# Two activation parts in one 512-column product, with the halves of the bank summed on VectorE

## The chip, the cores and the metric

The kernel runs on one core of one Trainium2 chip. The metric is the device time of one execution in microseconds. Engines are named as the profile names them: PE is TensorE (PEld its weight loads), DVE is VectorE, ACT is ScalarE, POOL is GpSimd, SP is SyncE. They run at once, each through its own list of instructions in order, and wait for one another on semaphores.

## The reference

Two transformer blocks over 256 tokens of width 1024, in float32. The change touches two places of the first block: the "up" half of its feed-forward layer (which runs twice, once in each of two layers) and the input projection of a short convolution.

```python
def dwconv3(x, w):
    xp = jnp.pad(x, ((0, 0), (1, 1), (0, 0)))
    return xp[:, :-2] * w[0] + xp[:, 1:-1] * w[1] + xp[:, 2:] * w[2]

def conv_ffn(a, w_up, conv_w, w_down):              # D_FF = 2816
    g, u = jnp.split(dwconv3(a @ w_up, conv_w), 2, axis=-1)
    return (jax.nn.silu(g) * u) @ w_down

def short_conv_mixer(a, w_in, conv_w, w_out):       # w_in is 1024 x 3072
    gate_b, gate_c, u = jnp.split(a @ w_in, 3, axis=-1)
    return (gate_b * dwconv3(gate_c * u, conv_w)) @ w_out
```

After this block come attention and a mixture of 32 experts, which take the second half of the time and which the change leaves alone.

## The kernel before, in words

**Products in three parts.** Activations lie transposed: 128 features on the partitions, 256 tokens along the free dimension, KC = 8 chunks of features. For precision each weight and each activation is split in two numbers, hi (rounded to fp32r) and lo (what is left), and a product is made as w_hi·a_hi + w_hi·a_lo + w_lo·a_hi, all summed in PSUM. `split_tile` makes one tile of 128 output features: for each of the 8 chunks a 256-column product with a_hi (L2127) and one with a_lo (L2128), then eight with w_lo (L2131). So w_hi's block is loaded twice for each chunk, and one tile is 24 products of 256 columns.

**Weight items.** Weights come by DMA in items of 1 MB (128 x 2048 in SBUF), into a ring of six cells. ACT rounds each item to `wd_hi` (`round_item`, L809) and DVE subtracts it to get `wd_lo` (`split_item`, L1337). Both have two buffers, so item k+2 can be split only when the tiles of item k are done, and the tile's L2131 products wait for DVE's part. One item holds the two tiles of one step of the loop below.

**The up loop** (`ffn` on each engine, FC = 22 steps j, two layers). Step j has a gate tile (s = 0) and a value tile (s = 1). PE makes both into two of six PSUM banks (`ffn_bank`). ACT multiplies each by the convolution's middle tap into SBUF (`center`, L961). DVE adds the two outer taps, shifted by one token, reading the tile from PSUM (`shifts`, L1561 and L1564, for the gate and then for the value). ACT takes the silu of the gate (L973), POOL multiplies gate and value (L742), ACT rounds that product (L955) and DVE makes its rest (L1554). The order within a step is written out by hand, and it is what the prediction is about. On ACT: center gate, center value, wait for the gate's two taps, silu, round weight item j+2, round the product of step j-1. On DVE: the four taps, the lo part of item j+2 (waits for ACT's rounding), the rest of step j-1. The last two steps split the first two items of the down half in place of up items.

**The short convolution** has 8 steps of three tiles (B, C and u): ACT copies C out of PSUM (L1000), DVE multiplies it with u (L1605), ACT applies the middle tap (L1004), DVE the outer ones (L1607, L1610), and DVE multiplies with B (L1616). In two of the steps DVE and ACT also split an item in the middle (`SC_BETWEEN`).

**The wide form** exists already for other matrices: `wide_tile` (L2144) multiplies w_hi with a_hi and a_lo side by side in one 512-column product, which fills a bank with two halves of 256 columns, and adds w_lo·a_hi to the second half (L2147). Whoever reads the tile adds the halves.

Of the kernel before, what the change touches and what calls it, by code (L numbers as in the profile page):

```python
# [129 lines left out]

SPLIT_STAGES = ("qkv", "win_out", "up0", "down0", "sc_in", "sc_out", "up1", "down1", "w_in", "w_out", "gate")
# [31 lines left out]
def build(nc, wdense, wmoe, small_d, tab_d, tab2_d, x_d, ctx_d, p_d, wg_d, wr_d, bup_d, bdown_d, out_d):  # L163
    with ExitStack() as stack:
# [136 lines left out]
        ctx_in, ctx_sq, ctx_sum, ctx_root = sem("ctx_in"), sem("ctx_sq"), sem("ctx_sum"), sem("ctx_root")  # L301
# [7 lines left out]
        FFN_COUNTS = dict(up=2 * FC, center=2 * FC, shift=4 * FC, silu=FC, act=FC, act_hi=FC, act_lo=FC, fed=9, right=KC, down=KC)  # L309
# [6 lines left out]
        sc_proj, sc_c, sc_cu, sc_center = sem("sc_proj"), sem("sc_c"), sem("sc_cu"), sem("sc_center")  # L316
        sc_shift, sc_mix, sc_out = sem("sc_shift"), sem("sc_mix"), sem("sc_out")

# [5 lines left out]
        def ffn_bank(j, s):  # L324
            return ps[:, 2 * (j % 3) + s, 0:T]
# [399 lines left out]
        def _(pool):  # L725
# [61 lines left out]
        def _(act):  # L787
# [57 lines left out]
            def window_qkv():  # L845
# [25 lines left out]
                def ctx_root_():  # L871
                    act.wait_ge(ctx_sum, 8)
                    act.activation(rstd[:, T:TT], ps[:, 6, 0:T], ACT.Sqrt, bias=eps[:, 0:1]).then_inc(ctx_root, 1)
# [76 lines left out]
            def ffn(L):  # L950
# [6 lines left out]
                def center(j, s):  # L957
                    act.wait_ge(*ffn_at(L, "up", j * 2 + s + 1))
                    if j >= 2:
                        act.wait_ge(*ffn_at(L, "act", j - 1))  # L960
                    act.activation(ffn_buf(s, j % 2), ffn_bank(j, s), ACT.Copy, scale=conv(L, 1, s)[:, j:j + 1]).then_inc(ffn_sem["center"], 1)  # L961

                bring_in(ACT.Silu, L)
                for j in range(FC):
# [7 lines left out]
                    act.wait_ge(*ffn_at(L, "shift", j * 4 + 2))  # L972
# [13 lines left out]
            def short_conv():  # L986
# [4 lines left out]
                for n in range(KC):  # L991
# [5 lines left out]
                    act.wait_ge(sc_proj, 3 * n + 1)  # L997
                    if n >= 2:
                        act.wait_ge(sc_mix, n - 1)
                    act.activation(sc_buf(0, b), ps[:, 3 * b, 0:T], ACT.Copy).then_inc(sc_c, 1)  # L1000
# [307 lines left out]
        def _(dve):  # L1308
# [46 lines left out]
            def norm(n, src=None, first=None):  # L1355
# [20 lines left out]
                if n == 5:  # L1376
                    dve.wait_ge(root_taken, 1)
# [20 lines left out]
            def window_qkv():  # L1398
# [37 lines left out]
                dve.wait_ge(ctx_root, 1)  # L1436
# [112 lines left out]
            def ffn(L, after):  # L1549
# [6 lines left out]
                def shifts(j):  # L1556
                    for s in range(2):
                        y, c = ffn_bank(j, s), ffn_buf(s, j % 2)
                        dve.wait_ge(*ffn_at(L, "center", j * 2 + s + 1))

                        dve.scalar_tensor_tensor(out=c[:, 1:T], in0=y[:, 0:T - 1], scalar=conv(L, 0, s)[:, j:j + 1], in1=c[:, 1:T],  # L1561
                                                 op0=ALU.mult, op1=ALU.add).then_inc(ffn_sem["shift"], 1)
                        dve.wait_ge(*ffn_at(L, "shift", j * 4 + 2 * s + 1))
                        dve.scalar_tensor_tensor(out=c[:, 0:T - 1], in0=y[:, 1:T], scalar=conv(L, 2, s)[:, j:j + 1], in1=c[:, 0:T - 1],  # L1564
                                                 op0=ALU.mult, op1=ALU.add).then_inc(ffn_sem["shift"], 1)

                split_item(up, 2)
# [21 lines left out]
            def short_conv():  # L1589
                def rest(n):  # L1590
# [3 lines left out]
                for n in range(KC):  # L1594
# [4 lines left out]
                    dve.wait_ge(sc_c, n + 1)  # L1599
# [4 lines left out]
                    cu, o = sc_buf(1, b), sc_buf(2, b)  # L1604
                    dve.tensor_tensor(cu, ps[:, 3 * b + 1, 0:T], sc_buf(0, b), ALU.mult).then_inc(sc_cu, 1)  # L1605
# [192 lines left out]
            def route():  # L1798
# [13 lines left out]
                dve.wait_ge(root_taken, 2)  # L1812
# [300 lines left out]
        def _(pe):  # L2113
# [160 lines left out]
            def window_qkv():  # L2274
# [75 lines left out]
                pe.wait_ge(ctx_root, 1)  # L2350
# [83 lines left out]
            def ffn(L):  # L2434
                up, down = f"up{L}", f"down{L}"
                first_tiles([ps[:, t, 0:T] for t in range(4)], up, (0, 1), ffn_sem["up"], NORM_GROUPS[2 * L + 1])
# [5 lines left out]
                pe.wait_ge(*ffn_at(L, "shift", 4 * (FC - 2)))  # L2442
                pe.wait_ge(mod_ready, modulated(NORM_GROUPS[2 * L + 1]))
                for j in range(11):
# [34 lines left out]
            def short_conv():  # L2479
                first_tiles([ps[:, t, 0:T] for t in range(4)], "sc_in", (0, 1), sc_proj, NORM_GROUPS[2])  # L2480
                for n in range(4, 24):
                    m, kind = n // 3, n % 3
                    if m >= 2 and kind == 0:
                        pe.wait_ge(sc_mix, m - 1)
# [676 lines left out]
```

## Time and profile before

| | |
|---|---|
| median of 3 runs | 1839.61 us (1839.33 to 1845.45) |
| the profiled execution: its span | 1841.9 us, inside the range of the runs and 2.3 us over their median |
| PE / DVE / ACT / POOL busy | 97% / 41% / 33% / 4% |
| granted PE clock, mean | 0.991 |
| two up loops, steady part | 99.08 us each, 17 steps |

A busy share is an average over stages with different limits, and the starts and ends of matmuls overlap, so it doesn't say what sets the time of a stage. The chain of waits does: it is followed back from the last instruction to what released each one.

### The profile page before, as it was taken

To read this page: it belongs to the slowest core of one execution; us is meant where nothing else is said; L and a number is where in the kernel's file an instruction comes from. 1 tells how busy PE (TensorE), PEld (TensorE's weight loads), DVE (VectorE), ACT (ScalarE), POOL (GpSimd) and SP (SyncE) were. 2 spreads that over 40 slices of the span, in tenths; PEclk is the share of its full clock that TensorE was granted. 3 is DMA by queue.
4 is the path that set the end of the run, shared out by engine and by line. 5 is a ranking of instruction groups with operands and counts; after the bars stand their busy time and mean duration, and the time that the engine had idled before them with its cause. 6 is when DMAs were issued, how large, how long until landed. Compare 5 with 4: busy or idle time off the path is not lost.

```text
span 1841.9 us, 32831 instructions
## 1 busy us (share of the span) xinstructions
PE 1790.2 (97%) x13696; PEld 1328.3 (72%) x13696; DVE 753.5 (41%) x1603; ACT 611.9 (33%) x1096; POOL 82.1 (4%) x98
## 2 busy tenths in 40 slices
PE   6999999999999999999999999999999999999997
PEld 4764899989899989968656656566656666556556
DVE  3575677656677746475211112121112112111116
ACT  3457555544455536484111111111111111111115
POOL 0010111100111100101000000000000000000001
PEclk9999999999999999989999999999999999999999
DMA  9648745556465464526899999999999999999993
GB/s 393 255 166 328 282 173 180 205 181 235 180 249 179 167 212 155 178 114 249 356 424 424 425 423 426 423 426 424 426 395 422 426 427 427 425 427 424 427 423 123
DMA packets 64421, 580.59 MB, mean 315 GB/s; under 512 B 5968, under 2 KB 9552, under 8 KB 11056
## 3 DMA queue, kind: packets, MB, share of 16 engines
q1 hardware_dynamic: 63872, 577.17, 77.5%
q8 instruction: 91, 1.49, 0.3%
q10 hardware_dynamic: 432, 1.71, 0.3%
q14 instruction: 26, 0.21, 0.0%
HBM read 577.81 MB, written 1.05 MB: 314 GB/s over the span
## 4 chain that ended last, share of the span: by engine, by line
PE 74%; DVE 11%; DMA 8%; ACT 6%; issue 1%; ACTq 0%; DVEq 0%; SPq 0%
PE ps L2807 22%; PE ps L2820 11%; DVE wd_lo L1337 6%; PE ps L2716 5%; ACT wd_hi L809 5%; DMA ring<-in_experts 4%; PE ps L2456 4%; DMA ring<-in_weights 3%; PE ps L2832 3%; PE ps L2460 2%; PE ps L2131 2%; PE ps L2127 2%; PE ps L2128 2%; PE ps L2205 2%; PE ps L2793 2%
## 5 line engine op out<-in xcount | busy, mean ns | idle before, releaser
L2807 PE MATMUL ps<-ring,A 128*64 128x256 f32 x3840 | 431.4, 381 | 7.8 <-DMA ring<-in_experts 3.8
L2807 PEld LDWEIGHTS ps<-ring,A 128*64 128x64 f32 x3840 | 272.4, 137 | 162.7 <-issue 25.3
L1980 DVE TENSOR_TENSOR A<-ps,W 128x512 f32<-128x512 f32 x64 | 44.3, 692 | 730.1 <-PE ps L2793 730.1
L1337 DVE TENSOR_TENSOR wd_lo<-ring,wd_hi 128x2048 fp32r<-128x2048 f32 x103 | 235.8, 2291 | 166.8 <-ACT wd_hi L809 166.7
L809 ACT ACTIVATE wd_hi<-ring 128x2048 fp32r<-128x2048 f32 x107 | 204.0, 1907 | 128.1 <-PE ps L2460 65.2
L2127 PE MATMUL ps<-aL_both,wd_hi 128*128 128x256 f32 x944 | 232.7, 284 | 1.9 <-ACT wd_hi L809 1.4
L2128 PE MATMUL ps<-aL_both,wd_hi 128*128 128x256 f32 x944 | 231.4, 283 | 0.0
L2820 PE MATMUL ps<-ring,A 128*64 128x512 f32 x960 | 213.4, 595 | 1.3 <-DMA ring<-in_experts 1.3
L2127 PEld LDWEIGHTS ps<-aL_both,wd_hi 128*128 128x128 f32 x944 | 181.0, 192 | 4.2 <-issue 3.1
L2128 PEld LDWEIGHTS ps<-aL_both,wd_hi 128*128 128x128 f32 x944 | 181.1, 192 | 0.1
L1155 ACT ACTIVATE A<-ps 128x512 f32<-128x512 f32 x64 | 38.2, 597 | 396.2 <-PE ps L2807 377.5
L2820 PEld LDWEIGHTS ps<-ring,A 128*64 128x64 f32 x960 | 66.5, 137 | 123.6 <-issue 121.6
L2131 PE MATMUL ps<-aL_both,wd_lo 128*128 128x256 f32 x944 | 135.7, 286 | 0.8 <-DVE wd_lo L1337 0.2
L2131 PEld LDWEIGHTS ps<-aL_both,wd_lo 128*128 128x128 f32 x944 | 120.8, 191 | 2.8 <-DVE wd_lo L1337 2.0
L2716 PE MATMUL ps<-A 128*128 128x64 f32 x960 | 113.9, 272 | 0.0
L2716 PEld LDWEIGHTS ps<-A 128*128 128x128 f32 x960 | 111.9, 192 | 0.0
L1203 ACT ACTIVATE A<-ps 128x512 f32<-128x512 f32 x32 | 19.1, 597 | 202.8 <-PE ps L2820 192.5
L1175 ACT ACTIVATE A<-A 128x256 f32<-128x256 f32 x64 | 26.7, 417 | 171.6 <-DVE A L1985 171.6
L2456 PE MATMUL ps<-ff_both,wd_hi 128*128 128x512 f32 x320 | 76.3, 391 | 0.0
L2456 PEld LDWEIGHTS ps<-ff_both,wd_hi 128*128 128x128 f32 x320 | 58.8, 188 | 11.4
L2832 PE MATMUL ps<-A 64*128 64x256 f32 x512 | 63.9, 389 | 1.3 <-ACT A L1203 1.3
L2832 PEld LDWEIGHTS ps<-A 64*128 64x128 f32 x512 | 47.0, 186 | 18.2 <-issue 14.1
(436 smaller groups left out, 2179.3 us busy)
## 6 DMA issues: line engine op xcount, KB each, us to landing
ring<-in_experts SPq DMA_DIRECT2D x180, 2048.0 KB, 20.8
ring<-in_weights SPq DMA_DIRECT2D x161, 1024.0 KB, 5.1
aT<-in_experts SPq DMA_DIRECT2D x11, 2048.0 KB, 20.4
hT<-in_x SPq DMA_DIRECT2D x1, 1024.0 KB, 7.4
hT<-in_ctx SPq DMA_DIRECT2D x1, 1024.0 KB, 18.4
hT<-in_weights SPq DMA_DIRECT2D x1, 1024.0 KB, 8.6
tab<-in_tables ACTq DMA_DIRECT2D x1, 768.0 KB, 7.0
tab<-in_experts SPq DMA_DIRECT2D x1, 768.0 KB, 4.4
```

The source lines that it names most:

```text
L809: act.activation(wd_hi[:, split_buf(name, k)], w, ACT.Copy).then_inc(split_hi, 1)
L1155: act.activation(u[:, j, :], ps[:, 4 + j, :], ACT.Copy).then_inc(moe["u"], 1)
L1337: dve.tensor_tensor(wd_lo[:, b], cell(PLAN[name]["first"][k]["cell"]), wd_hi[:, b].bitcast(F32), ALU.subtract).then_inc(split_lo, 1)
L1980: dve.tensor_tensor(m_gl[:, j].rearrange("p c h n -> p (c h) n"), ps[:, TURN_BANKS[j], :].rearrange("p (c n) -> p c n", c=8), b_up[:, 8 * ...
L2127: pe.matmul(out, wd_hi[:, b, c, cols], a_hi[:, c, :], start=(c == 0), stop=False)
L2128: pe.matmul(out, wd_hi[:, b, c, cols], a_lo[:, c, :], start=False, stop=False)
L2131: mm = pe.matmul(out, wd_lo[:, b, c, cols], a_hi[:, c, :], start=False, stop=(c == KC - 1))
L2456: pe.matmul(halves(n), hi[:, k, n * P:(n + 1) * P], ff_both[:, :, kk], start=(kk == 0), stop=False)
L2716: mm = pe.matmul(ps[:, GATHER_BANK, c * CAP:(c + 1) * CAP], xt[:, s, c * P:(c + 1) * P], oh[:, s, :], start=(s == 0), stop=(s == 1))
L2807: mm = pe.matmul(ps[h * CAP:(h + 1) * CAP, 4 + j, q * T:(q + 1) * T], xg[:, c, :], block(c, h), start=(c == 0), stop=(c == KC - 1))
L2820: mm = pe.matmul(ps[h * CAP:(h + 1) * CAP, DOWN_BANK, :], m_act[:, 4 * kh + c, :], w[:, c, h], start=(kh == 0 and c == 0), stop=(kh == 1 a ...
L2832: mm = pe.matmul(ps[:, f // 2, (f % 2) * T:(f % 2 + 1) * T], y[rows, n * P:(n + 1) * P], ohT[rows, :], start=(first and n % 2 == 0), stop= ...
```

## The change

Up tiles and convolution input tiles are made with `wide_tile` (and `first_tiles` with wide=True for the first four): 8 products of 512 columns and 8 of 256 for each tile, in place of 24 of 256. The two halves of the bank are added by a DVE reduction out of PSUM into SBUF. In the up loop `center` and the taps then read that sum, and the value's two outer taps move from DVE to POOL, each as a tensor_scalar and a tensor_tensor, since POOL can't read PSUM. In the short convolution three DVE sums take the place of ACT's copy, and the two products with a PSUM operand read SBUF.

```diff
@@ PE
             def ffn(L):
...
-                        pe.wait_ge(*ffn_at(L, "shift", 4 * (j - 2)))
+                        pe.wait_ge(*up_summed(L, 2 * (j - 2)))
                     for s in range(2):
-                        split_tile(ffn_bank(j, s), up, j, s, aL_hi, aL_lo, ffn_sem["up"])
+                        wide_tile(ffn_bank(j, s), up, j, s, aL_both, ffn_sem["up"])
@@ DVE
-                def shifts(j):
+                def sums_and_shifts(j):
                     for s in range(2):
-                        y, c = ffn_bank(j, s), ffn_buf(s, j % 2)
-                        dve.wait_ge(*ffn_at(L, "center", j * 2 + s + 1))
-
-                        dve.scalar_tensor_tensor(out=c[:, 1:T], in0=y[:, 0:T - 1], scalar=conv(L, 0, s)[:, j:j + 1], in1=c[:, 1:T],
+                        dve.wait_ge(*ffn_at(L, "up", j * 2 + s + 1))
+                        if j >= 1:
+                            dve.wait_ge(*(ffn_at(L, "shift_value", 4 * j) if s else ffn_at(L, "shift", 2 * j)))
+                        dve.tensor_reduce(ffn_up(s), ps[:, ffn_bank(j, s), :].rearrange("p (i t) -> p t i", i=2), AX_X, ALU.add).then_inc(summed, 1)
+                    dve.wait_ge(*ffn_at(L, "center", j * 2 + 1))
+                    gate = ffn_buf(0, j % 2)
+                    for i, (tap, to, of) in enumerate(TAPS):
+                        dve.scalar_tensor_tensor(out=gate[:, to], in0=ffn_up(0)[:, of], scalar=conv(L, tap, 0)[:, j:j + 1], in1=gate[:, to],
                                                  op0=ALU.mult, op1=ALU.add).then_inc(ffn_sem["shift"], 1)
...
@@ ACT
-                    act.wait_ge(*ffn_at(L, "up", j * 2 + s + 1))
+                    act.wait_ge(*up_summed(L, j * 2 + s + 1))
...
-                    act.activation(ffn_buf(s, j % 2), ffn_bank(j, s), ACT.Copy, scale=conv(L, 1, s)[:, j:j + 1]).then_inc(ffn_sem["center"], 1)
+                    act.activation(ffn_buf(s, j % 2), ffn_up(s), ACT.Copy, scale=conv(L, 1, s)[:, j:j + 1]).then_inc(ffn_sem["center"], 1)
@@ POOL
                 for j in range(FC):
+                    pool.wait_ge(*ffn_at(L, "center", j * 2 + 2))
+                    value = ffn_buf(1, j % 2)
+                    for i, (tap, to, of) in enumerate(TAPS):
+                        pool.tensor_scalar(tap_of_value[:, to], ffn_up(1)[:, of], conv(L, tap, 1)[:, j:j + 1], None, ALU.mult).then_inc(ffn_sem["shift_value"], 1)
+                        pool.wait_ge(*ffn_at(L, "shift_value", 4 * j + 2 * i + 1))
+                        pool.tensor_tensor(value[:, to], value[:, to], tap_of_value[:, to], ALU.add).then_inc(ffn_sem["shift_value"], 1)
+                        pool.wait_ge(*ffn_at(L, "shift_value", 4 * j + 2 * i + 2))
                     pool.wait_ge(*ffn_at(L, "silu", j + 1))
-                    pool.wait_ge(*ffn_at(L, "shift", j * 4 + 4))
@@ DVE, short convolution
-                    dve.wait_ge(sc_c, n + 1)
+                    dve.wait_ge(sc_proj, 3 * n + 1)
+                    both_halves(sc_buf(0, b), 3 * b)
...
-                    dve.tensor_tensor(cu, ps[:, 3 * b + 1, 0:T], sc_buf(0, b), ALU.mult).then_inc(sc_cu, 1)
+                    both_halves(cu, 3 * b + 1)
+                    dve.wait_ge(*sc_summed(3 * n + 2))
+                    dve.tensor_tensor(cu, cu, sc_buf(0, b), ALU.mult).then_inc(sc_cu, 1)
```

DVE's list in the up loop, one step in the steady part (from the weight item's lo part to the next one; W is the small SBUF buffer, ps PSUM). Before:

```order
L1337 TENSOR_TENSOR wd_lo<-ring,wd_hi 128x2048
L1554 TENSOR_TENSOR ff_both<-A,ff_both 128x256
L1561 SCALAR_TENSOR_TENSOR W<-ps,small,W 128x255
L1564 SCALAR_TENSOR_TENSOR W<-ps,small,W 128x255
L1561 SCALAR_TENSOR_TENSOR W<-ps,small,W 128x255
L1564 SCALAR_TENSOR_TENSOR W<-ps,small,W 128x255
```

And now the same step and the start of the next:

```order
L1356 TENSOR_TENSOR wd_lo<-ring,wd_hi 128x2048
L1573 TENSOR_TENSOR ff_both<-A,ff_both 128x256
L1580 TENSOR_REDUCE W<-ps 128x256 x2
L1584 SCALAR_TENSOR_TENSOR W<-W,small 128x255 x2
L1356 TENSOR_TENSOR wd_lo<-ring,wd_hi 128x2048
```

Two sums stand where the gate's taps stood, the gate's taps follow them, and the value's taps are gone; the taps read SBUF now.

POOL's list in the up loop, one step before (22 of them follow one another):

```order
L742 TENSOR_TENSOR A<-W 128x256 [waits ffn_shift,ffn_silu] x22
```

And one step now:

```order
L757 TENSOR_SCALAR rstd<-W,small 128x255 [waits ffn_center]
L759 TENSOR_TENSOR W<-W,rstd 128x255 [waits ffn_shift_value]
L757 TENSOR_SCALAR rstd<-W,small 128x255 [waits ffn_shift_value]
L759 TENSOR_TENSOR W<-W,rstd 128x255 [waits ffn_shift_value]
L763 TENSOR_TENSOR A<-W 128x256 [waits ffn_silu,ffn_shift_value]
```

One instruction of a step became five, four of which wait for the one before them.

## Rows read from the trace of the kernel before

**Rows 1.** The page: busy time of each engine, and the whole chain by engine

```profile
PE 1790.2 (97%) x13696; PEld 1328.3 (72%) x13696; DVE 753.5 (41%) x1603; ACT 611.9 (33%) x1096; POOL 82.1 (4%) x98
...
PE 74%; DVE 11%; DMA 8%; ACT 6%; issue 1%; ACTq 0%; DVEq 0%; SPq 0%
```

**Rows 2.** Busy time, steady part of layer 0's up loop: span, then PE, PEld, DVE, ACT, POOL

```profile
236.99:336.07 99.08, 98.94 (x814) 98.38 (x814) 74.42 (x102) 57.06 (x86) 12.62 (x17) 1.00 0.50 179
```

**Rows 3.** The chain of waits through layer 0's up loop: shares, then start, length, what

```profile
by line: DVE wd_lo L1337 35.5%; ACT wd_hi L809 28.3%; DVE W L1564 9.1%; DVE W L1561 7.6%; DVE ff_both L1554 5.1%; issue 5.0%; PE ps L2165 2.0%; PE ps L2164 1.9%; PE ps L2460 1.6%; PE ps L2171 1.4%; PE ps L2456 1.2%; ACTq L960 0.5%; ACT W L9
...
236.99 2.29 DVE wd_lo L1337
...
336.07 2.29 DVE wd_lo L1337
```

**Rows 4.** Timeline of DVE in one step: start, length, instruction, [idle before, releaser]

```profile
291.99 0.48 DVE L1561 SCALAR_TENSOR_TENSOR W<-ps,small,W 128x255 f32<-128x255 f32 x1
292.50 0.48 DVE L1564 SCALAR_TENSOR_TENSOR W<-ps,small,W 128x255 f32<-128x255 f32 x1
...
295.27 2.29 DVE L1337 TENSOR_TENSOR wd_lo<-ring,wd_hi 128x2048 fp32r<-128x2048 f32 x1 [1.38 <-ACT wd_hi L809]
297.48 0.42 DVE L1554 TENSOR_TENSOR ff_both<-A,ff_both 128x256 fp32r<-128x256 f32 x1
297.82 0.48 DVE L1561 SCALAR_TENSOR_TENSOR W<-ps,small,W 128x255 f32<-128x255 f32 x1
```

**Rows 5.** Timeline of ACT in the same step

```profile
293.02 0.42 ACT L973 ACTIVATE W<-W 128x256 f32<-128x256 f32 x1 [2.45 <-DVE W L1564]
293.34 1.90 ACT L809 ACTIVATE wd_hi<-ring 128x2048 fp32r<-128x2048 f32 x1
```

**Rows 6.** Timeline of PE in the up loop: a tile's first and last parts

```profile
300.59 1.12 PE L2131 MATMUL ps<-aL_both,wd_lo 128*128 128x256 f32 x8
301.55 0.28 PE L2127 MATMUL ps<-aL_both,wd_hi 128*128 128x256 f32 x1
...
303.47 0.72 PE L2131 MATMUL ps<-aL_both,wd_lo 128*128 128x256 f32 x4
```

**Rows 7.** Timeline of PE in the attention's output projection, which has wide tiles

```profile
193.03 2.00 PE L2144 MATMUL ps<-aL_both,wd_hi 128*128 128x512 f32 x8
194.87 0.40 PE L2147 MATMUL ps<-aL_both,wd_lo 128*128 128x256 f32 x2
```

**Rows 8.** Groups by line and shape, whole run: busy us, mean ns of one

```profile
L1635 DVE COPY A<-ps 128x512 f32<-128x512 f32 x2 | 1.4, 692 | 2.7 <-PE ps L2185 2.7
...
L1907 DVE TENSOR_REDUCE A<-A 128x21 f32<-128x672 f32 x1 | 0.9, 854 | 0.0
...
L734 POOL COPY A<-A 64x512 f32<-64x512 f32 x8 | 4.9, 610 | 106.8 <-DVE A L1408 106.5
```

**Rows 9.** POOL's instruction of the up loop: ns min/median/max

```profile
L742 POOL TENSOR_TENSOR A<-W x44: 732/742/2647, 229.0 to 642.1; 128x256 f32<-128x256 f32 x44
```

**Rows 10.** Timeline of POOL at the last step of layer 0

```profile
344.32 2.64 POOL L742 TENSOR_TENSOR A<-W 128x256 f32<-128x256 f32 x1 [2.90 <-DVE W L1564]
```

**Rows 11.** Timeline of DVE at the same place

```profile
344.09 2.28 DVE L1337 TENSOR_TENSOR wd_lo<-ring,wd_hi 128x2048 fp32r<-128x2048 f32 x1
346.29 0.95 DVE L1554 TENSOR_TENSOR ff_both<-A,ff_both 128x256 fp32r<-128x256 f32 x1
```

**Rows 12.** Timeline of POOL where each addition waits for the one before

```profile
201.06 1.62 POOL L749 TENSOR_TENSOR sq<-sq,aT 128x256 f32<-128x256 f32 x2
```

**Rows 13.** Timeline of DVE at the start of layer 0's loop, item 3's lo part

```profile
230.63 2.28 DVE L1337 TENSOR_TENSOR wd_lo<-ring,wd_hi 128x2048 fp32r<-128x2048 f32 x1
```

**Rows 14.** Timeline of DVE in the short convolution, a lo part between two products

```profile
445.90 2.29 DVE L1337 TENSOR_TENSOR wd_lo<-ring,wd_hi 128x2048 fp32r<-128x2048 f32 x1
```

**Rows 15.** The chain of waits through the short convolution

```profile
448.68 0.96 PE ps L2131 x8
...
481.43 0.42 DVE A L1616
```

More of the change, by code:

```diff
@@ L308, in build @@
         wo_out = sem("wo_out")
-        FFN_COUNTS = dict(up=2 * FC, center=2 * FC, shift=4 * FC, silu=FC, act=FC, act_hi=FC, act_lo=FC, fed=9, right=KC, down=KC)
+        FFN_COUNTS = dict(up=2 * FC, center=2 * FC, shift=2 * FC, shift_value=4 * FC, silu=FC, act=FC, act_hi=FC, act_lo=FC, fed=9, right=KC, down=KC)
         ffn_sem = {k: sem("ffn_" + k) for k in FFN_COUNTS}
@@ L314, in ffn_at, with up_summed, sc_summed @@
             return ffn_sem[name], FFN_COUNTS[name] * L + value
-        sc_proj, sc_c, sc_cu, sc_center = sem("sc_proj"), sem("sc_c"), sem("sc_cu"), sem("sc_center")
+        sc_proj, summed, sc_cu, sc_center = sem("sc_proj"), sem("summed"), sem("sc_cu"), sem("sc_center")
         sc_shift, sc_mix, sc_out = sem("sc_shift"), sem("sc_mix"), sem("sc_out")
+        def up_summed(L, value):
+            return summed, (2 * FC + SC_SUMS) * L + value
+        def sc_summed(value):
+            return summed, 2 * FC + value
         def ffn_buf(kind, b):
@@ L324, in ffn_bank, with ffn_up @@
         def ffn_bank(j, s):
-            return ps[:, 2 * (j % 3) + s, 0:T]
+            return 2 * (j % 3) + s
+        def ffn_up(s):
+            return ffn_buf(3, s)
+        TAPS = ((0, slice(1, T), slice(0, T - 1)), (2, slice(0, T - 1), slice(1, T)))
+        tap_of_value = rstd[:, T:TT]
         def conv(L, tap, s):
@@ L872, in ctx_root_ @@
                     act.wait_ge(ctx_sum, 8)
-                    act.activation(rstd[:, T:TT], ps[:, 6, 0:T], ACT.Sqrt, bias=eps[:, 0:1]).then_inc(ctx_root, 1)
+                    act.activation(rstd[:, T:TT], ps[:, 6, 0:T], ACT.Sqrt, bias=eps[:, 0:1]).then_inc(root_taken, 1)
                 query(0)
@@ L996, in short_conv @@
                         mixed(n - 1)
[L997 to L1000, printed above, removed]
                     if n in SC_BETWEEN:
@@ L1003, in short_conv @@
                     act.wait_ge(sc_cu, n + 1)
+                    if n >= 2:
+                        act.wait_ge(sc_mix, n - 1)
                     act.activation(sc_buf(2, b), sc_buf(1, b), ACT.Copy, scale=vec("sc_conv", 8 + n, 9 + n)).then_inc(sc_center, 1)
@@ L1589, in short_conv, with both_halves @@
             def short_conv():
+                def both_halves(out, bank):
+                    dve.tensor_reduce(out, ps[:, bank, :].rearrange("p (i t) -> p t i", i=2), AX_X, ALU.add).then_inc(summed, 1)
                 def rest(n):
@@ L2435, in ffn @@
                 up, down = f"up{L}", f"down{L}"
-                first_tiles([ps[:, t, 0:T] for t in range(4)], up, (0, 1), ffn_sem["up"], NORM_GROUPS[2 * L + 1])
+                first_tiles(range(4), up, (0, 1), ffn_sem["up"], NORM_GROUPS[2 * L + 1], wide=True)
                 for j in range(2, FC):
                     if j >= 3:
-                        pe.wait_ge(*ffn_at(L, "shift", 4 * (j - 2)))
+                        pe.wait_ge(*up_summed(L, 2 * (j - 2)))
                     for s in range(2):
-                        split_tile(ffn_bank(j, s), up, j, s, aL_hi, aL_lo, ffn_sem["up"])
-                pe.wait_ge(*ffn_at(L, "shift", 4 * (FC - 2)))
+                        wide_tile(ffn_bank(j, s), up, j, s, aL_both, ffn_sem["up"])
+                pe.wait_ge(*up_summed(L, 2 * (FC - 2)))
                 pe.wait_ge(mod_ready, modulated(NORM_GROUPS[2 * L + 1]))
@@ L2479, in short_conv @@
             def short_conv():
-                first_tiles([ps[:, t, 0:T] for t in range(4)], "sc_in", (0, 1), sc_proj, NORM_GROUPS[2])
+                first_tiles(range(4), "sc_in", (0, 1), sc_proj, NORM_GROUPS[2], wide=True)
                 for n in range(4, 24):
```

36 lines of the change are left out of this document (19 added, 17 removed).

## The prediction

> **What bounds the kernel now.** I read the page first. PE is busy 97% of the span and carries 74% of the chain [rows 1], so a change that shortens products looks like a gain. But the change works in two up loops and a short convolution only, so I asked there. In the steady part of layer 0's up loop PE counts as busy 98.94 of 99.08 us, DVE 74.42, ACT 57.06 [rows 2]. The chain of waits over the same loop says otherwise: its parts are DVE's lo split (35.5%), ACT's rounding (28.3%), DVE's taps and rest, and hardly a matmul [rows 3]. The reader is to see that a full PE share hides a loop that others pace. Lo parts start at 236.99 and 336.07, 17 steps apart [rows 3], so a step is 99.08/17 = 5.83 us.
>
> That is exactly one round of DVE and ACT, each link starting when the one before ends [rows 4, 5]: gate tap 291.99 to 292.50 (0.51), second tap to silu 293.02 (0.52), silu to rounding 293.34 (0.32), rounding to lo part 295.27 (1.93), lo part to rest 297.48 (2.21), rest to the next tap 297.82 (0.34). Sum 5.83. PE's own need: w_lo's eight products take 301.55 - 300.59 = 0.96, the sixteen with w_hi 303.47 - 301.55 = 1.92 [rows 6]; two tiles 5.76. PE is 0.07 us a step short of being the bound, the ring is the bound.
>
> **PE's part of the change.** A 512-column product takes (194.87 - 193.03)/8 = 0.23 us [rows 7] against 2 x 0.12 [rows 6]. The second weight load that disappears was hidden already. A wide tile is 1.84 + 0.96 = 2.80 us against 2.88: a step of the up loop would need 5.60. As the ring sets the step, this saves nothing there. The first four tiles of each stage are PE-paced, 32 pairs x 0.01 = 0.3 us, three stages: -1.0.
>
> **Two sums join the ring.** A PSUM read of 512 columns on DVE is 692 ns; a reduction of 672 columns is 854 [rows 8], 160 columns more for 0.16 us, so a sum of 512 is 0.69. Back to back an instruction costs some 0.08 less than its length (2.29 against 2.21, 0.42 against 0.34, rows 4), so 0.61 each. The value's taps leave DVE, but they ran beside ACT's silu and rounding, where DVE afterwards still sat idle 1.38 us [rows 4]: taking them away gains nothing. The sums stand ahead of the gate's taps, on the path: 5.83 + 2 x 0.61 = 7.05. ACT's value center (about 0.45 behind the second sum) is done before the two taps are, so it doesn't lengthen it. Taps from SBUF in place of PSUM I leave at 0.51.
>
> **POOL joins in.** How POOL and DVE share is seen at layer 0's end. POOL's product, normally 742 ns [rows 9], took 2.64 from 344.32 because DVE's lo part ran to 346.37 (two SBUF operands); it ended 346.96, 0.59 after it. DVE's rest, due at 346.29, then took 0.95 in place of 0.42 [rows 4, 10, 11]. So each kept the other out. In the steady steps before, the product fell into DVE's idle time. Dependent POOL additions follow each other after 1.62 - 0.74 = 0.88 us [rows 12].
> The Trainium skill says it as a rule (SBUF — State Buffer, "SBUF: two separate sides"): the pair of ports that the two engines share is an exclusive lock for a whole instruction. Perfetto Trace Analysis, "Optimizing Scalar/DVE Operations", warns that moving work between these two might not help. The trace agrees with the first (2.64 and 0.95 us); the second is what this change does.
>
> Now POOL has four taps and the product. The additions cost 0.88. A one-input tensor_scalar on 255 columns isn't in the trace; below it lies half of POOL's copy of 512 columns, 0.35 with a start, above it the two-input 0.74 [rows 8, 9]; I take 0.5, nearer the copy, which has one input too. Time from the start of the first sum: sums 0 to 1.29, value center ready 1.75, gate's taps 1.22 to 2.2, silu, rounding, lo part due 4.5. POOL's first tap waits for the gate's second (two SBUF operands now) and ends 2.54. Then addition 2.68 to 3.42, tap 3.56 to 4.06, addition 4.20 to 4.94. The lo part, due 4.5, waits 0.44 for it. POOL's product then waits out the lo part and holds the rest back, as in the rows: +0.53. Step: 7.05 + 0.44 + 0.53 = 8.02. With the tap at 0.35 the lo part waits 0.15 only (7.7); with 0.74 the last addition comes after the lo part begins (7.6). If POOL wins the lock ahead of the gate's second tap, that costs 0.4 and POOL is through in time for the rest: 7.7. I take 7.8, inside 7.6 to 8.0; without any collision 7.05.
>
> **Start and end of the loop.** ACT's center of the first step now waits for a DVE sum that stands behind item 2's lo part, and item 3's rounding stands behind it on ACT: item 3's lo part goes from 230.63 [rows 13] to about 232.4, +1.8. The next lo part came 6.36 later (236.99); at 7.8 that is +1.4. At the end two sums of the last step and a collision stand in front of the down half's first lo part: +1.0. The down half follows at once, with PE as its bound, so nothing is made up.
> One layer: 17 x (7.8 - 5.83) = 33.5, + 1.8 + 1.4 + 1.0 = 37.7. Two: 75.4.
>
> **The short convolution.** Its chain is matmuls, 2.88 apart (448.68 is one of them) [rows 15]; here PE does bound. 20 wide tiles x 0.08 = -1.6. Against it: the third sum of the last step lies between the last tile and DVE's product at 481.43, +0.6. In the two steps with a lo part in the middle that part ends 445.90 + 2.29 = 448.19 [rows 14], PE wants it 448.68: 0.49 to spare. The second sum delays it by 0.69 and a semaphore (0.07), PE comes 0.16 sooner: 0.43 late, twice, +0.9. Net -0.1. POOL has nothing here.
>
> **Sum.** 75.4 - 1.0 - 0.1 = +74. The profiled span would be 1841.9 + 74 = 1916; the median lies 2.3 lower, so 1914.
>
> **The rivals.** A difference of 0.5% (9 us) is about what this kernel's measurement can tell from none.
> 1. Sums and collisions pace the up loops, step 7.6 to 8.0: for 7.6, 17 x 0.2 x 2 less and 0.4 from the start, 1907; for 8.0, 1921. Chance 0.55.
> 2. Only the sums count: POOL always slips in. Step 7.05: 17 x 1.22 = 20.7, start 1.8 + 0.7, end 0.6, 23.8 a layer, 1839.6 + 46.5 = 1886. For it: POOL was never in the way in the steady steps. Against: its work was 0.74 a step, now some 3.5 with waits, in an idle time of DVE of 2.3. Steps between give the times between. Chance 0.15.
> 3. POOL itself becomes the ring: the second sum waits for POOL's fourth tap of the step before. Sum 0.69, center 0.45, two additions 1.76, two taps with their waits, and a lo part in between (2.2). It passes 7.8 when a POOL tap takes over 1.2 us; at a step of 8.6, 17 x 0.8 x 2 more: 1943. Nothing in the trace speaks for so slow a tap. Chance 0.12.
> 4. Faster: the DVE-ACT round is no real bound, because DVE can take its sums while it waits, and PE's tiles set the step. Then 17 x 0.23 x 2 = 7.8 saved, with 1.0 and 0.1: 1831. It decides if the round falls under 5.60; it was 5.83 with four links that all remain. For it only PE's full share. Chance 0.08; with half-hidden sums it gives no change.
> 5. PE now idles some 2 us a step. Its granted clock is 1.00 in the loop [rows 2]. If the pauses brought it to the lower level (1.2 GHz), a step's products, 5.60 at the higher, would near 11 and set it: beyond 1990. Chance 0.03.
> The Trainium skill's page TensorE: Matmul & The Clock Gate ties the lower level to idle gaps; no row here shows such a pause in the loop.
>
> **How the numbers follow.** Predicted is case 1's 1914. What is left, 0.07, is half-hidden sums: steps around 6.3, 1855 to 1870. The range of 8 in 10 takes cases 1 and 2 and the near half of case 3: 1884 to 1936. Faster 0.06, same 0.04, slower 0.90.
>
> **What would show it.** In the changed profile: steps of 7.6 to 8.0 between lo parts; DVE's reductions 0.69; the silu some 1.2 later after the rest than now; POOL additions of 742 ns, some of 1 to 3 us; rests near 0.95; matmuls of 0.23; PE share of the loop under 80%; the convolution's stage within 1 us of now. It is wrong if sums start while DVE waits for ACT, if the reduction takes far from 0.69 (each 0.1 moves the result by 17 x 2 x 2 x 0.1 = 7 us), or if POOL's spans show no blocking.

## The result and the profile after

The changed kernel takes 1926.46 us (median of 6 runs, 1924.61 to 1931.78), the kernel before 1845.33 (median of 6 runs, 1839.33 to 1849.88; three of them are those with the median of 1839.61 that the prediction started from). The medians differ by 81 us and the profiled spans by 80.9. The ratio, 1.0463 with a 95% interval of 1.0446 to 1.0479, puts it at 85 us (82 to 88). The predicted direction, the range and the loop that pays are right. The sum of +74 was 7 us short by the medians and 11 by the ratio; the forecast of 1914 was 12.5 us under the median, as 5.7 of it is the starting value. One term of the sum, the short convolution, had the wrong mechanism.

The page after, busy time by engine and the chain by engine:

```profile
PE 1796.4 (93%) x12800; PEld 1275.6 (66%) x12800; DVE 805.2 (42%) x1627; ACT 617.2 (32%) x1088; POOL 305.5 (16%) x274
...
PE 65%; DVE 10%; DMA 10%; ACT 7%; issue 5%; POOL 2%; DVEq 0%; ACTq 0%; SPq 0%; POOLq 0%
```

POOL went from 82 to 306 us, PE's part of the chain from 74% to 65% [rows 1]. The steady part of layer 0's up loop, again 17 steps, between the lo parts of items 4 and 21 (span, then PE, PEld, DVE, ACT, POOL, and the granted clock):

```profile
243.41:373.12 129.71, 103.39 (x544) 83.22 (x544) 90.28 (x102) 60.26 (x86) 102.77 (x86) 1.00 0.41 138
```

It was 99.08 us [rows 2]. PE now counts as busy 80% of it (103.39 of 129.71), at a granted clock of 1.00 still. The chain of waits through the same stretch:

```profile
by line: issue 31.1%; ACT wd_hi L830 24.9%; DVE W L1580 16.7%; DVE W L1584 12.8%; DVE ff_both L1573 9.5%; DVE wd_lo L1356 4.7%; ACT W L994 0.3%; ACTq L981 0.2%
```

No matmul is in it; before, there was hardly one [rows 3]. The new part is L1580, the two sums. Its 31% of "issue" hides lo parts: the chain books 1.87 of the 2.29 us of most lo parts as issue here. One step on DVE (start, length, instruction; x2 where two follow each other):

```profile
304.47 2.29 DVE L1356 TENSOR_TENSOR wd_lo<-ring,wd_hi 128x2048 fp32r<-128x2048 f32 x1 [2.29 <-ACT wd_hi L830]
306.68 0.95 DVE L1573 TENSOR_TENSOR ff_both<-A,ff_both 128x256 fp32r<-128x256 f32 x1
307.55 1.28 DVE L1580 TENSOR_REDUCE W<-ps 128x256 f32<-128x512 f32 x2
308.81 1.00 DVE L1584 SCALAR_TENSOR_TENSOR W<-W,small 128x255 f32<-128x255 f32 x2
312.10 2.29 DVE L1356 TENSOR_TENSOR wd_lo<-ring,wd_hi 128x2048 fp32r<-128x2048 f32 x1 [2.29 <-ACT wd_hi L830]
```

and on ACT:

```profile
309.85 0.42 ACT L994 ACTIVATE W<-W 128x256 f32<-128x256 f32 x1 [0.47 <-DVE W L1584]
310.17 1.90 ACT L830 ACTIVATE wd_hi<-ring 128x2048 fp32r<-128x2048 f32 x1
```

The round closes as before [rows 4, 5], with more in it: lo part 2.21, rest 0.87 (was 0.34), two sums 1.26, two taps to the silu 1.04, silu 0.32, rounding 1.93. Sum 7.63, and the lo parts are 312.10 - 304.47 = 7.63 apart, in every step. Of the 1.80 us that a step grew, 1.26 are the sums and 0.53 is the rest, which now takes 0.95. POOL in the same step says why:

```profile
301.84 1.15 POOL L757 TENSOR_SCALAR rstd<-W,small 128x255 f32<-128x255 f32 x1 [1.24 <-ACT W L982]
303.07 0.73 POOL L759 TENSOR_TENSOR W<-W,rstd 128x255 f32<-128x255 f32 x1
303.89 0.93 POOL L757 TENSOR_SCALAR rstd<-W,small 128x255 f32<-128x255 f32 x1
304.91 2.44 POOL L759 TENSOR_TENSOR W<-W,rstd 128x255 f32<-128x255 f32 x1
307.42 0.81 POOL L763 TENSOR_TENSOR A<-W 128x256 f32<-128x256 f32 x1
```

The second addition starts 0.44 us after the lo part did, waits it out, ends at 307.35 (0.59 after the lo part's end), and the rest, due 306.68, ends only behind it. This is the pair of rows that stood once at the end of each layer before [rows 10, 11], now in every step. The Trainium skill (SBUF — State Buffer, "SBUF: two separate sides") calls the ports that the two share an exclusive lock held for a whole instruction; the trace agrees in that each keeps the other out, with 2.44 and 0.95 us in 17 of 17 steps. It doesn't show a clean hand-over: the addition ends 0.59 us after the lo part, and alone it takes 0.73.

PE in the same place:

```profile
304.58 2.08 PE L2174 MATMUL ps<-aL_both,wd_hi 128*128 128x512 f32 x8 [1.39 <-ACT wd_hi L830]
306.81 1.22 PE L2177 MATMUL ps<-aL_both,wd_lo 128*128 128x256 f32 x8 [0.16 <-DVE wd_lo L1356]
```

Its products come at the pace that was read ahead [rows 6, 7], and it waits 1.39 us a step for the rounded weight item and 0.16 for its lo part.

### The profile page after: what moved, and what is told of

Read it like the earlier page. It is cut to its first block, busy times and chain, and to the rows that moved or that the text cites. A ratio compares the mean times of both kernels' runs of the same rounds, so it can differ in the third digit from the quotient of the medians.

```text
span 1922.8 us, 31307 instructions
## 1 busy us (share of the span) xinstructions
PE 1796.4 (93%) x12800; PEld 1275.6 (66%) x12800; DVE 805.2 (42%) x1627; ACT 617.2 (32%) x1088; POOL 305.5 (16%) x274
## 3 DMA queue, kind: packets, MB, share of 16 engines
q8 instruction: 84, 1.38, 0.3%
## 4 chain that ended last, share of the span: by engine, by line
PE 65%; DVE 10%; DMA 10%; ACT 7%; issue 5%; POOL 2%; DVEq 0%; ACTq 0%; SPq 0%; POOLq 0%
PE ps L2837 20%; PE ps L2850 9%; DMA ring<-in_experts 7%; ACT wd_hi L830 5%; PE ps L2746 5%; DMA ring<-in_weights 3%; PE ps L2486 3%; DVE W L1580 3%; PE ps L2862 3%; DVE wd_lo L1356 2%; PE ps L2174 2%; DVE W L1584 2%; PE ps L2235 2%; PE ps L2490 2%; PE ps L2192 2%
## 5 line engine op out<-in xcount | busy, mean ns | idle before, releaser
L2174 PE MATMUL ps<-aL_both,wd_hi 128*128 128x512 f32 x848 | 219.7, 402 | 49.5 <-ACT wd_hi L830 49.0
L2174 PEld LDWEIGHTS ps<-aL_both,wd_hi 128*128 128x128 f32 x848 | 154.6, 192 | 84.9 <-issue 55.2
L2177 PEld LDWEIGHTS ps<-aL_both,wd_lo 128*128 128x128 f32 x848 | 113.8, 193 | 40.8 <-DVE wd_lo L1356 35.7
L2177 PE MATMUL ps<-aL_both,wd_lo 128*128 128x256 f32 x848 | 124.1, 289 | 16.7 <-DVE wd_lo L1356 16.1
L759 POOL TENSOR_TENSOR W<-W,rstd 128x255 f32<-128x255 f32 x88 | 129.2, 1469 | 7.4
L757 POOL TENSOR_SCALAR rstd<-W,small 128x255 f32<-128x255 f32 x88 | 99.6, 1132 | 95.1 <-ACT W L982 90.7
L982 ACT ACTIVATE W<-W,small 128x256 f32<-128x256 f32 x88 | 44.9, 510 | 153.5 <-DVE W L1580 145.2
```

Of the source, the lines that this page charges most:

```text
L757: pool.tensor_scalar(tap_of_value[:, to], ffn_up(1)[:, of], conv(L, tap, 1)[:, j:j + 1], None, ALU.mult).then_inc(ffn_sem["shift_value"], 1)
L759: pool.tensor_tensor(value[:, to], value[:, to], tap_of_value[:, to], ALU.add).then_inc(ffn_sem["shift_value"], 1)
L2174: pe.matmul(halves(bank), wd_hi[:, b, c, cols], parts[:, :, c, :], start=(c == 0), stop=False)
L2177: mm = pe.matmul(ps[:, bank, T:TT], wd_lo[:, b, c, cols], parts[:, 0, c, :], start=False, stop=(c == KC - 1))
```

## The experiments

Ten kernels. Steps are distances of lo parts on DVE in the steady part of layer 0's up loop. They repeat within 0.03 us, but for one step of 7.53 with the rest before the lo part and one of 7.69 with the rounding ahead in the new kernel; in the two old kernels with the rounding ahead the first four steps are shorter (4.89 to 5.59). They are the sharper measure, since single runs of one kernel spread by up to 0.7%. "New" is the changed kernel, "old" the one before. Ratios are to the old kernel's runs taken together with each.

| kernel | base | step, us | median, us | ratio to old (95%) |
|---|---|---|---|---|
| old | | 5.83 | 1841 to 1845 | |
| new | | 7.63 | 1926.5 | 1.0463 (1.0446 to 1.0479) |
| value taps on DVE | new | 7.10 | 1900.2 | 1.0309 (1.0280 to 1.0339) |
| pairs of 256 columns | new | 7.63 | 1929.3 | 1.0471 (1.0442 to 1.0499) |
| rest before the lo part | new | 7.18 | 1910.3 | 1.0370 (1.0338 to 1.0403) |
| convolution alone | old | 5.83 | 1847.7 | 1.0037 (1.0020 to 1.0054) |
| rounding ahead of silu | old | 5.76 | 1838.4 | 0.9973 (0.9958 to 0.9988) |
| value taps on DVE, rounding ahead | new | 6.74 | 1886.9 | 1.0232 (1.0201 to 1.0263) |
| wide products, no sums | old | 5.83 | 1840.3 | 0.9987 (0.9970 to 1.0004) |
| wide, no sums, rounding ahead | old | 5.59 | 1832.7 | 0.9938 (0.9914 to 0.9962) |
| rounding ahead | new | 7.34 | 1916.4 | 1.0393 (1.0358 to 1.0427) |
| taps on DVE, rounding ahead, rest first | new | 5.98 | 1858.7 | 1.0081 (1.0052 to 1.0111) |

**Value taps back on DVE.**

```diff
@@ POOL
-                    for i, (tap, to, of) in enumerate(TAPS):
-                        pool.tensor_scalar(tap_of_value[:, to], ffn_up(1)[:, of], ...)
...
-                        pool.tensor_tensor(value[:, to], value[:, to], tap_of_value[:, to], ALU.add)
...
@@ DVE, behind the gate's taps
+                    for i, (tap, to, of) in enumerate(TAPS):
+                        dve.scalar_tensor_tensor(out=value[:, to], in0=ffn_up(1)[:, of], scalar=conv(L, tap, 1)[:, j:j + 1], in1=value[:, to],
+                                                 op0=ALU.mult, op1=ALU.add)
...
```

> The changed kernel with the value's two outer taps on VectorE again, behind the gate's; GpSimd keeps only the product. Theory A (GpSimd's work costs by keeping VectorE's rest out, 0.53 us a step, and by its backlog at the loop's start and end): the value's taps (0.9 us) fit into VectorE's 2.29 us of idle time before the lo part, steps go from 7.63 to about 7.1, 17 of them save 9 us a layer, start and end 4 to 7 more: 1926 - 26 to 32, about 1897. Rival B (VectorE is the scarce engine): the taps lengthen the round, step 7.63 - 0.53 + 0.9 = 8.0, about 1938. Rival C (GpSimd doesn't matter): steps stay 7.63, 1926.

Measured 1900.2 us. DVE in one step:

```profile
302.26 1.00 DVE L1585 SCALAR_TENSOR_TENSOR W<-W,small 128x255 f32<-128x255 f32 x2
304.63 2.29 DVE L1350 TENSOR_TENSOR wd_lo<-ring,wd_hi 128x2048 fp32r<-128x2048 f32 x1 [1.37 <-ACT wd_hi L824]
306.84 0.42 DVE L1567 TENSOR_TENSOR ff_both<-A,ff_both 128x256 fp32r<-128x256 f32 x1
```

The value's taps lie in the wait for ACT, which shrinks from 2.29 to 1.37 us, and the round doesn't grow by them. The rest is 0.42 again: 7.63 - 0.53 = 7.10. Theory A holds; the taps were moved off an engine that had the time, onto one that keeps it waiting. The start and the end of the loop tell more: the distances of lo parts there, 9.58, 9.66 and 10.42 us in the new kernel, are 8.66, 7.63 and 9.33 here, so POOL's taps cost 0.9, 2.0 and 1.1 us at these places in each layer.

**Pairs of 256 columns in the new kernel.** The edit in `wide_tile`, for the up tiles and the convolution's:

```diff
-                    pe.matmul(halves(bank), wd_hi[:, b, c, cols], parts[:, :, c, :], start=(c == 0), stop=False)
+                    if name in ("up0", "up1", "sc_in"):
+                        for i in range(2):
+                            pe.matmul(ps[:, bank, i * T:(i + 1) * T], wd_hi[:, b, c, cols], parts[:, i, c, :], start=(c == 0), stop=False,
...
```

The numbers that this kernel returns are not the reference's, and no run shows why, so it stands for its time alone.

> The changed kernel with every 512-column product of the up tiles (steps 2 on) and convolution tiles (fifth on) made as two of 256 columns into the same halves; everything on the other engines stays. Theory A (the round of VectorE and ScalarE paces the up loop and the first steps of the convolution): no difference in the up loops, steps stay 7.63; the convolution's last steps give +0.08 a tile, +1 us in all. Rival (the wide product saves 0.08 to 0.11 us a tile everywhere): 100 tiles, +8 to +11 us, and steps of 7.8.

Steps 7.63, to the hundredth. The median is 2.8 us over the new kernel's, with intervals that overlap. What the change was about, the wide product, gives nothing in the up loops of the new kernel.

**The rest ahead of the lo part**, in the new kernel.

```diff
@@ ACT
                     if 1 < j < FC - 2:
+                        rounded(j - 1)
                         round_item(up, j + 2)
...
-                    if j >= 1:
+                    if j == 1 or j >= FC - 2:
                         rounded(j - 1)
@@ DVE
+                    if 1 < j < FC - 2:
+                        rest(j - 1)
                     if 0 < j < FC - 2:
                         split_item(up, j + 2)
...
-                    if j >= 1:
+                    if j == 1 or j >= FC - 2:
                         rest(j - 1)
```

> The changed kernel with ScalarE's rounding of the last step's product put ahead of its weight rounding, and VectorE's rest of it ahead of the lo part, into its idle time. Theory A (the rest costs 0.34 + 0.53 us because GpSimd's blocked addition runs right behind the lo part): both leave the round, 0.31 us joins it on ScalarE, steps 7.63 - 0.87 + 0.31 = 7.07, 17 x 2 x 0.56 = 19 us less, about 1907. Rival (the 0.53 belongs to no collision with the rest): only 0.34 leaves and 0.31 comes, steps stay 7.6, 1926.

```profile
301.14 2.29 DVE L1357 TENSOR_TENSOR wd_lo<-ring,wd_hi 128x2048 fp32r<-128x2048 f32 x1 [1.38 <-ACT wd_hi L830]
303.35 1.47 DVE L1581 TENSOR_REDUCE W<-ps 128x256 f32<-128x512 f32 x2
304.73 1.00 DVE L1585 SCALAR_TENSOR_TENSOR W<-W,small 128x255 f32<-128x255 f32 x2
306.52 0.43 DVE L1574 TENSOR_TENSOR ff_both<-A,ff_both 128x256 fp32r<-128x256 f32 x1 [0.79 <-ACT ff_both L976]
```

7.18 against 7.07 expected and 7.6 of the rival. The rest takes 0.43 and is hidden. The 0.11 that is missing shows in the sums: from the first one to the taps it is now 304.73 - 303.35 = 1.38 us, and was 1.26. The second sum must wait for POOL's last addition, which ends at 304.02, when the first sum is just done (303.35 + 0.68).

**The convolution's change alone, on the old kernel.** Of the diff shown ahead, the part of `short_conv` on the three engines.

```diff
@@ PE
-                    split_tile(ps[:, 3 * (m % 2) + kind, 0:T], "sc_in", n // 2, n % 2, aL_hi, aL_lo, sc_proj)
+                    wide_tile(3 * (m % 2) + kind, "sc_in", n // 2, n % 2, aL_both, sc_proj)
@@ DVE
+                    both_halves(sc_buf(0, b), 3 * b)
...
+                    both_halves(cu, 3 * b + 1)
...
+                    both_halves(sc_buf(3, b), 3 * b + 2)
...
```

> The kernel before with the change of the short convolution alone. Theory A (in the first three steps, which give one weight item each, VectorE's round went from 5.0 to 6.9 us and passes PE's 5.6 for an item): about 3.7 us more than the kernel before, steps of 6.9 at first. Rival (as predicted blind: PE paces the whole convolution): within 0.5 us of the kernel before.

```profile
429.73 2.28 DVE L1339 TENSOR_TENSOR wd_lo<-ring,wd_hi 128x2048 fp32r<-128x2048 f32 x1
431.93 1.28 DVE L1593 TENSOR_REDUCE W<-ps 128x256 f32<-128x512 f32 x2
433.24 0.42 DVE L1613 TENSOR_TENSOR W<-W 128x256 f32<-128x256 f32 x1
434.25 0.48 DVE L1615 SCALAR_TENSOR_TENSOR W<-W,small 128x255 f32<-128x255 f32 x1 [0.58 <-ACT W L1006]
...
435.17 0.68 DVE L1593 TENSOR_REDUCE W<-ps 128x256 f32<-128x512 f32 x1
435.95 0.43 DVE L1626 TENSOR_TENSOR A<-W 128x256 f32<-128x256 f32 x1
...
436.63 2.28 DVE L1339 TENSOR_TENSOR wd_lo<-ring,wd_hi 128x2048 fp32r<-128x2048 f32 x1
```

436.63 - 429.73 = 6.90 us for a step that makes one weight item, without an idle moment but the 0.58; in the old kernel such a step took 5.0 (lo parts at 428.05 and 433.07). PE wants an item each 5.6. From the lo part ahead of the stage to the one behind it the stage takes 70.23 us against 66.57, +3.7, and the profiled spans are 1845.5 and 1841.9, +3.6. The ratio of 1.0037 would be 6.8 us with an interval of 3.7 to 9.9, so the traces' figure lies at its low edge; the rival's 0.5 is out by both.

**Rounding ahead of silu, in the old kernel.** One swap on ACT in the up loop:

```diff
+                    if 1 < j < FC - 2:
+                        round_item(up, j + 2)
                     act.wait_ge(*ffn_at(L, "shift", j * 4 + 2))
                     act.activation(ffn_buf(2, b), ffn_buf(0, b), ACT.Silu).then_inc(ffn_sem["silu"], 1)
-                    if 1 < j < FC - 2:
-                        round_item(up, j + 2)
```

> The kernel before with one swap on ScalarE in the up loop: the rounding of weight item j+2 stands ahead of the gate's silu, no longer behind it. Theory A (a round of VectorE and ScalarE of 5.83 us paces the loop, PE needs 5.76): the rounding no longer waits for VectorE's taps, PE becomes the bound, steps of 5.76, 17 x 2 x 0.07 = 2.4 us less than the kernel before. Rival (PE paced the loop already, as its busy share says): no change.

The chain of waits through its up loop is all PE now:

```profile
by line: PE ps L2131 34.0%; PE ps L2127 33.1%; PE ps L2128 33.1%
```

Steps of 5.76, the 24 x 2 products of 0.12. This is the measured answer to "what bounds the loop before": the DVE-ACT round did, by 0.07 us a step, and PE's own time stands right behind it. At 0.9973 (0.9958 to 0.9988), 2 to 8 us less, it is also a version that beats both kernels, if by little.

**The same swap where the value's taps are on DVE**, both edits on the new kernel.

```diff
@@ ACT, beside the taps' edit above
+                    if 1 < j < FC - 2:
+                        round_item(up, j + 2)
                     act.wait_ge(*ffn_at(L, "shift", j * 2 + 2))
                     act.activation(ffn_buf(2, b), ffn_buf(0, b), ACT.Silu).then_inc(ffn_sem["silu"], 1)
```

> The changed kernel with the value's taps on VectorE and the same swap on ScalarE. Theory A: the round is then sum, sum, value center, rounding, lo part, rest; the rounding starts 0.9 us earlier than with the taps on VectorE alone, steps 7.10 - 0.9 = 6.2, 30 us less than that one's 1900: about 1870. Rival (PE or the tile buffers bound by now): steps of 7.1 stay, 1900.

6.74 against the expected 6.2. The swap does take the silu and the taps out of the round, but:

```profile
300.43 2.29 DVE L1350 TENSOR_TENSOR wd_lo<-ring,wd_hi 128x2048 fp32r<-128x2048 f32 x1 [0.48 <-ACT wd_hi L824]
302.63 0.96 DVE L1567 TENSOR_TENSOR ff_both<-A,ff_both 128x256 fp32r<-128x256 f32 x1
```

```profile
300.84 2.47 POOL L757 TENSOR_TENSOR A<-W 128x256 f32<-128x256 f32 x1 [4.28 <-ACT W L990]
```

The silu now ends right after the lo part begins, so POOL's product (its one instruction) falls behind the lo part and holds the rest back, 0.96 for 0.42. 6.2 and 0.54 are the 6.74. The 0.9 us that the swap was to give did come; I had forgotten to ask where the product would land.

**Wide products without sums**, in the old order and with the swap. The taps and centers read the second half of the bank only, so w_hi·a_hi is left out of the result, and both kernels stand for their time alone.

```diff
-            return ps[:, 2 * (j % 3) + s, 0:T]
+            return ps[:, 2 * (j % 3) + s, T:TT]
...
-                        split_tile(ffn_bank(j, s), up, j, s, aL_hi, aL_lo, ffn_sem["up"])
+                        wide_tile(2 * (j % 3) + s, up, j, s, aL_both, ffn_sem["up"])
```

> The kernel before with the up tiles as 512-column products but without any sum of the halves: taps and centers read the second half of the bank alone, so the part w_hi times a_hi is left out of the result. What the wide form gives when its sums cost nothing. Theory A: the round of VectorE and ScalarE holds steps at 5.83; only the first four tiles of each layer gain, 0.3 us each: within 1 us of the kernel before. Rival (the gain was there and the sums ate it): 88 tiles x 0.08 to 0.11, 7 to 10 us less.

> The same with the swap on ScalarE (rounding ahead of silu), again without the sum of the halves. Theory A: with the round out of the way PE's tiles set the step, 5.60, 17 x 2 x 0.23 = 7.8 us less than the kernel before, and 0.6 for the first tiles: -8.4. Rival (512-column products don't pace a stage faster than pairs of 256): the same as the swap alone, -2.4.

Steps 5.83 in the first, with the same chain as the old kernel; 5.59 in the second, whose chain is PE's alone:

```profile
by line: PE ps L2144 66.5%; PE ps L2147 33.9%
```

So the wide form is worth (5.76 - 5.59) = 0.17 us a step where PE is the bound, some 6 us in both loops, and nothing where the round is. Even free of sums it would have shown nothing here. The first of the two also prices the sums: beside the new kernel with its taps on DVE it lacks them and little else (the taps read SBUF there and PSUM here), and 7.10 - 5.83 = 1.27 us is the 1.26 that they take in the timeline. So the step is built up in runs: 5.83, 7.10 with the sums, 7.63 with the taps on POOL.

**The swap in the new kernel**, the value's taps still on POOL: the ACT lines of the diff two experiments up, without the taps' edit.

> The changed kernel, GpSimd keeping the value's taps, with the one swap on ScalarE (weight rounding ahead of silu). Theory A (GpSimd's own chain is a second bound close behind: value center, scale, add, scale, add, one of them held behind the lo part, and only then VectorE's next value sum): VectorE's round alone would allow 6.75, GpSimd's chain takes 7.1 to 7.2, so steps of about 7.15 and 16 us less, 1910. Rival (only VectorE and ScalarE matter, as in the kernel without GpSimd's taps): steps of 6.75, 30 us less, 1896.

7.34, not 7.15 and not 6.75. Here POOL's chain is the bound, as theory A says (POOL has 89% of the chain of waits from 250 to 340 us); its parts:

```profile
301.73 3.12 POOL L757 TENSOR_SCALAR rstd<-W,small 128x255 f32<-128x255 f32 x1
304.93 0.73 POOL L759 TENSOR_TENSOR W<-W,rstd 128x255 f32<-128x255 f32 x1
```

```profile
305.76 0.69 DVE L1580 TENSOR_REDUCE W<-ps 128x256 f32<-128x512 f32 x1 [1.04 <-POOL W L759]
```

The second scale is the one that the lo part (301.49) holds, and a blocked scale ends later than a blocked addition: at 304.85, 1.07 us after the lo part's end, where the addition took 0.59. DVE then waits 1.04 us for POOL's last addition before it may make the value's sum.

**All three remedies.** On top of the taps on DVE and the swap:

```diff
@@ ACT, head of the step
+                    if 1 < j < FC - 2:
+                        rounded(j - 1)
                     for s in range(1 if j == FC - 1 else 0, 2):
                         center(j, s)
@@ DVE, ahead of the lo part
+                    if 1 < j < FC - 2:
+                        rest(j - 1)
```

> The kernel with the value's taps on VectorE and weight rounding ahead of silu (steps of 6.74, 1887 us), and now the last product's rounding at the head of ScalarE's step and its rest on VectorE ahead of the lo part. Theory A (in that kernel GpSimd's product starts right behind the lo part's start, waits it out in 2.47 us and keeps the rest out, 0.96 in place of 0.42): 0.87 leaves the round, steps of 5.87, 34 x 0.87 = 30 us less, about 1857, and the up loop costs no more than before the change. Rival (VectorE is full: sums, four taps, lo part and rest are 5.7 and waits come on top): steps of 6.3 or more, 1872 or more.

```profile
302.61 0.42 ACT L970 ACTIVATE ff_both<-A 128x256 fp32r<-128x256 f32 x1 [2.65 <-POOL A L757]
302.93 0.89 ACT L976 ACTIVATE W<-W,small 128x256 f32<-128x256 f32 x2
303.73 1.90 ACT L824 ACTIVATE wd_hi<-ring 128x2048 fp32r<-128x2048 f32 x1
```

```profile
299.69 2.29 DVE L1352 TENSOR_TENSOR wd_lo<-ring,wd_hi 128x2048 fp32r<-128x2048 f32 x1
...
305.67 2.29 DVE L1352 TENSOR_TENSOR wd_lo<-ring,wd_hi 128x2048 fp32r<-128x2048 f32 x1
```

5.98 against 5.87, the rival's 6.3 is out. What bounds the step is a new round, which the expectation hadn't seen. POOL's product starts behind the lo part and waits it out until 302.57; ACT's rounding of that product, at the head of its step, waits for it; the centers and the weight rounding stand behind: 2.92 from the lo part to the rounding of the product, 0.32, 0.80 for the centers and 1.94 from the weight rounding to the next lo part, sum 5.98. The rival's premise was near, though: DVE's own list fills 5.70 of the 5.98, and it waits only 0.28, for the centers. The up loop is then within 0.15 us a step of the old one, with both sums in it, at 1.0081 (1.0052 to 1.0111) of the old kernel, 15 us. Of the 85 us by the ratio some four fifths were thus a matter of where and in which order the work was put. But the order helps the old kernel too (1838.4 with one swap), and with the sums the wide form still doesn't win.

## Why the prediction was right, and where it was not

- **The bound of the loop** (a round of DVE and ACT at 5.83, PE at 5.76 behind it): right. The swap in the old kernel gave 5.76.
- **PE's part saves nothing** in the up loop: right (7.63 with pairs, 5.83 with wide products and no sums). The 0.23 us of a 512-column product held, and so did the 0.3 us of the first tiles (the second lo part to the third: 5.48 us, was 5.79).
- **Two sums on the path, 2 x 0.61**: right, 1.26 in the timeline and 1.27 between two kernels.
- **The value's taps were free on DVE**: right. Back there they cost nothing.
- **POOL keeps the rest out, +0.53**: right, shown by 0.95 against 0.42 and by both kernels that take the collision away (7.10 and 7.18). This term and the backlog of POOL at the start and end told 1886 from 1914, and case 1 held over case 2.
- **The lo part held back by POOL's last addition, +0.44**: it didn't happen. The missing price was that of POOL's scale. I took 0.5 us; it is 0.93 alone and 1.15 behind the gate's taps, so the last addition comes 0.44 after the lo part began. The sentence "with 0.74 the last addition comes after the lo part begins (7.6)" is what happened; the taken 7.8 was 0.17 too high, which made the steady part 33.5 in place of 30.7 us a layer.
- **Start and end of the loop**: too small, and this more than made up for it. Per layer I had 1.8, 1.4 and 1.0. Measured by distances of lo parts: item 2's to item 3's 9.58 against 5.88, +3.7; to item 4's 9.66 against 6.36, +3.3; the last lo part to the down half's first 10.42 against 8.02, +2.4. In all three DVE waits for POOL, which the prediction had named as case 3's mechanism and had left out here:

```profile
232.23 0.69 DVE L1580 TENSOR_REDUCE W<-ps 128x256 f32<-128x512 f32 x1 [2.79 <-POOL W L759]
...
239.52 0.69 DVE L1580 TENSOR_REDUCE W<-ps 128x256 f32<-128x512 f32 x1 [2.35 <-POOL W L759]
...
382.07 0.69 DVE L1580 TENSOR_REDUCE W<-ps 128x256 f32<-128x512 f32 x1 [2.76 <-POOL W L759]
```

  Where two steps follow each other without a lo part between, the second value sum must wait for four POOL instructions. In the middle one a lo part lies between, but POOL's first scale waited it out (last section). POOL is less than half of the 9.4, however: with the value's taps on DVE the same distances are still 8.66, 7.63 and 9.33, 5.4 us over the old kernel's. That part is the sums: four at the start, where two steps stand together (2.8), two in the middle (1.3), and four at the end, where some fall into a wait (1.3). I had 4.2 for all. Sum of a layer: 30.7 + 3.7 + 3.3 + 2.4 = 40.1 against 37.7.
- **The short convolution, -0.1**: wrong, +3.7 in the new kernel (70.26 us against 66.57 between the lo parts around it). The step that failed is "here PE does bound", said of the whole stage from the chain of the old kernel. It bound there, and DVE had only 0.7 us to spare in the first steps: a step was 5.0 us on DVE and PE's item 5.76. Three sums of 0.61 make 6.9. I had priced the sums only in the two steps with a lo part in the middle and at the stage's end.
- **The sum**: from its second lo part to the down half's first a layer takes 164.90 us against 125.13, which is the 40.1 less 0.3 for the first tiles. Two layers are 79.5, the down halves behind them 0.8 each, the convolution 3.7: together 84.9. Of this 1.7 us comes back in the first items of the second block, and ACT's first copy of that block's projections starts at 813.8 against 730.8, +83.0. The spans differ by 80.9; where the last 2 us go is not shown.
- **Luck**: that +74 came within 7 to 11 us is partly luck. The steps were 5.6 us too dear in both layers, and the starts and ends 10.4 and the convolution 3.8 us too cheap; the errors have different causes and stand against each other by chance.
- **A lower clock by PE's pauses** (case 5): did not come; 1.00 is granted in the loop, with a pause of 1.39 us a step.

## What to carry to other kernels

Before a faster instruction is put into a stage, ask which round of waits has the stage's period: add up the starts of one step around the engines, and if they close exactly, only what stands in that round counts, whatever an engine's busy share says. Then ask of every stage apart how much the engine behind the bound has to spare, with the work the change adds. Work is free in another engine's wait and dear ahead of it. Between VectorE and GpSimd the price is not the instruction but where it lands: here a GpSimd addition of 0.73 us that started behind a VectorE one of 2.29 took 2.44, and then held the next VectorE one back by 0.53 us, in every step.

## What the runs showed of the hardware

POOL's tensor_scalar on 255 columns of float32 with a scalar per partition takes longer than its two-input addition, though it reads one tensor less (nanoseconds, min/median/max):

```profile
L757 POOL TENSOR_SCALAR rstd<-W,small x88: 932/1029/3197, 228.3 to 731.4; 128x255 f32<-128x255 f32 x88
...
L759 POOL TENSOR_TENSOR W<-W,rstd x88: 721/734/2528, 229.5 to 732.4; 128x255 f32<-128x255 f32 x88
```

I had expected it below the addition's 0.74. To start ahead of the lo part doesn't save such a scale. At the loop's start one began 0.19 us before it and still ended 0.73 us behind it, while the lo part kept its length:

```profile
233.56 3.20 POOL L757 TENSOR_SCALAR rstd<-W,small 128x255 f32<-128x255 f32 x1 [0.63 <-ACT W L982]
```

```profile
233.75 2.28 DVE L1356 TENSOR_TENSOR wd_lo<-ring,wd_hi 128x2048 fp32r<-128x2048 f32 x1
```

The reductions over two halves of a PSUM bank, a stride of 256 columns, took 678 ns in the middle, close to the 692 of a copy of 512 contiguous columns [rows 8].
